# Scores joined over two halves of the key positions, a rewritten routing and placement, and all gathers of the combine issued first

## What is computed

```python
# MLA, per head: 128 "nope" features and 64 "rope" features, causal softmax over 1024 keys
s = (einsum('bqhd,bkhd->bhqk', qn, k_nope) + einsum('bqhr,bkr->bhqk', qp, k_pe)) * scale
p = softmax(where(mask, s, -inf));  out = einsum('bhqk,bkhe->bqhe', p, v)
# experts: top group of 4, top 2 experts of its 4; 2048 assignments in all
g_sel = argmax(g_logits);  e_top, e_idx = top_k(e_logits[g_sel], 2)
gate = softmax(g_logits)[g_sel] * softmax(e_top)
expert_id = g_sel * 4 + e_idx
counts = bincount(expert_id);  pad_start = cumsum(pad(counts)) - pad(counts)
dest = pad_start[e] + rank of the assignment within its expert
ys = (silu(xs @ w_gate[e]) * (xs @ w_up[e])) @ w_down[e]    # xs gathered by block
out[tok] = gate0 * ys[dest0] + gate1 * ys[dest1];  result = rms_norm(h + out)
```

## Time and profile before

| | us |
|---|---|
| median of 3 runs | 3902.52 (3900.98 to 3903.48) |
| the profiled execution, own time | 3896.27 |
| its span, first to last instruction | 3895.0 |
| PE busy | 3660.8 (94%) |
| DVE busy | 1771.2 (45%) |
| ACT busy | 1017.9 (26%) |
| POOL busy | 693.2 (18%) |
| mean granted TensorE clock | 0.973 |

### The profile page before, as it was taken

One profiled execution on the slowest core, in us unless ns is written; L12 is line 12 of the kernel. 1 busy time (PEld: TensorE's weight loads), 2 busy tenths in 40 slices (PEclk: granted clock), 3 DMA queues, 4 the chain that ended last, 5 costly groups with the idle time before them and its releaser, 6 DMA issues. The chain is left out here.

```text
span 3895.0 us, 42152 instructions
## 1 busy us (share of the span) xinstructions
PE 3660.8 (94%) x16927; PEld 2372.2 (61%) x16927; DVE 1771.2 (45%) x3356; ACT 1017.9 (26%) x1857; POOL 693.2 (18%) x688
## 2 busy tenths in 40 slices
PE   5999999999999989998999999999898896999994
PEld 4666554777777766665547888888663553333331
DVE  5666754455555536666333334444326633000003
ACT  2444223322222214443223222222120411111111
POOL 1122000110000002211001111000010002555554
PEclk9999899999999999999999999999999997999997
DMA  6010550222222140002411111111400204887524
GB/s 213 29 33 21 190 172 27 68 76 81 80 88 90 51 159 25 25 24 85 151 33 44 44 44 54 44 44 43 132 3 0 94 28 158 311 292 254 204 82 146
DMA packets 226147, 364.55 MB, mean 94 GB/s; under 512 B 54584, under 2 KB 156690, under 8 KB 213664
## 3 DMA queue, kind: packets, MB, share of 16 engines
q1 hardware_dynamic: 175440, 239.22, 18.3%
q0 software_dynamic: 47232, 121.75, 8.8%
q10 hardware_dynamic: 3280, 0.89, 0.1%
HBM read 519.00 MB, written 44.04 MB: 145 GB/s over the span
## 5 line engine op out<-in xcount | busy, mean ns | idle before, releaser
L225 PE MATMUL psum<-arena_r,arena_r 128*128 128x512 f32 x4096 | 1302.5, 397 | 15.7 <-DVE weight_ring_r L1775 14.7
L225 PEld LDWEIGHTS psum<-arena_r,arena_r 128*128 128x128 f32 x4096 | 770.5, 188 | 204.5 <-issue 17.4
L225 PE MATMUL psum<-arena 64*128 64x128 f32 (+9 forms) x4048 | 859.4, 382 | 33.4 <-DVE arena L3074 14.9
L225 PEld LDWEIGHTS psum<-arena 128*128 128x128 f32 (+1 forms) x4048 | 521.7, 194 | 335.8 <-issue 220.6
L1801 DVE TENSOR_TENSOR arena<-arena,psum 128x512 f32<-128x512 f32 x512 | 336.7, 684 | 189.4 <-PE psum L225 189.4
L225 PE MATMUL psum<-weight_ring_r,arena_r 128*128 128x512 f32 x1024 | 410.5, 401 | 0.0
L225 PE MATMUL psum<-arena_r,weight_ring_r 128*128 128x512 f32 x1024 | 398.5, 389 | 0.0
L225 PE MATMUL psum<-arena,weight_ring 128*128 128x512 f32 x768 | 341.1, 604 | 19.7 <-DVE arena L2266 12.6
L1758 POOL TENSOR_TENSOR weight_ring_r<-weight_ring,arena_r 128x1024 fp32r<-128x1024 f32 x64 | 154.7, 2419 | 1129.3 <-ACT arena_r L1708 1129.3
L3186 PE MATMUL psum<-arena 128*64 128x512 f32 x1536 | 341.7, 598 | 3.9 <-DMA arena<-in_expert_w_gate,be_i 2.5
L1792 DVE TENSOR_TENSOR arena_r<-arena,arena_r 128x512 fp32r<-128x512 f32 x128 | 88.5, 691 | 462.8 <-ACT arena_r L1746 462.8
(11 more groups left out here) (378 smaller groups left out, 3343.7 us busy)
## 6 DMA issues: line engine op xcount, KB each, us to landing
weight_ring<-in_w_mlp_up SPq DMA_DIRECT2D x32, 1024.0 KB, 6.3
weight_ring<-in_w_mlp_down SPq DMA_DIRECT2D x32, 1024.0 KB, 4.9
arena<-in_w_ada SPq DMA_DIRECT2D x24, 1024.0 KB, 6.0
arena<-in_w_ada SPq DMA_DIRECT2D x40, 512.0 KB
arena<-in_w_in SPq DMA_DIRECT2D x6, 2048.0 KB, 18.5
tmp_ys<-arena SPq DMA_DIRECT2D x24, 512.0 KB
arena<-in_w_out SPq DMA_DIRECT2D x4, 2048.0 KB, 9.2
arena<-tmp_mixed SPq DMA_DIRECT2D x16, 512.0 KB, 3.3
```

What stands on the lines that cost most here:

```text
L225: i = self.nc.tensor.matmul(out, lhs, rhs, start=start and n == 0, stop=stop and n == len(pairs) - 1)
```

## The change

- In attention the key features `kpeT` of tiles 4 to 7 stand on partitions 64 to 127, and the query features `qpeT` on both halves. `pe_scores` first does the 128-row products of both 512-column parts, then the two 64-row products, one on each half of the rows. `sp_queries` and `sp_first_queries` issue one more transfer per head. In the last tile of a mixer VectorE makes a doubled copy (`first_q`) before TensorE turns it.
- The route drops an operation from each `dve_first_max`, builds `hot` by products of one-hots, sums with one scan over tiles (`upto`), and takes the counts and the places from separate products. The gate weights (`dve_route_gates`) come after the placement. Four tables are made in the route's loop (`dve_route_tables`).
- The placement computes `dest` first and the experts of the blocks after it; `row_hot` is made in two halves; the 16 products are 32 columns wide and write four partial sums on four groups of partitions, which a copy and a product with `fold` add up.
- `pool_experts` gathers the rows of step 0 before the gate weights of step 0.
- The combine issues all 16 gathers first; VectorE takes six tiles before it scales the first.

```diff
     V.rt = A.take(2, MH + 1, HALF_ROPE)
+    V.first_q = V.rt.rearrange("p a h f -> p (a h f)")[:, 0:P]
     A = Area(k.arena, 0)
...
         E.wait_ge(read.at("rot", l, t), made.at("ga", l, t + 1) if more else made.at("q_up", l, t, 1))
-        k.turn([(ps[0][0:ROPE, at(h)], V.pe_rot[:, h, :]) for h in range(MH)]).then_inc(*out.up("turn_qpe", l, t))
+        turned = [(ps[0][0:ROPE, at(h)], V.pe_rot[:, h, :]) for h in range(MH)]
+        if not more:
+            E.wait_ge(read.at("first_q", l))
+            turned[0] = (ps[0][:, at(0)], V.first_q)
+        k.turn(turned).then_inc(*out.up("turn_qpe", l, t))
         E.wait_ge(made.at("qk", l, t + 1) if more else made.at("kv", l, t, 0))
-        k.turn([(ps[1][0:ROPE, 0:P], V.pe_rot[:, MH, :])]).then_inc(*out.up("turn_kpe", l, t))
+        if t < NT // 2:
+            k.turn([(ps[1][0:ROPE, 0:P], V.pe_rot[:, MH, :])]).then_inc(*out.up("turn_kpe", l, t))
+        else:
+            k.turn([(ps[1][:, 0:P], flat(V.pe_rot[:, MH - 1:MH + 1, :]))]).then_inc(*out.up("turn_kpe", l, t))
         if more:
...
         if not more:
-            s.activation(k.att.qpeT[0][0:ROPE, at(t)], k.ps[0][0:ROPE, 0:P], ACT.Copy)
+            s.activation(k.att.qpeT[0][:, at(t)], k.ps[0][:, 0:P], ACT.Copy)
         s.activation(V.qpe_out[0:ROPE].rearrange("p h n -> p (h n)"), k.ps[0][0:ROPE], ACT.Copy).then_inc(*out.up("qpe", l, t))
         E.wait_ge(pe.at("turn_kpe", l, t))
         if more:
             E.wait_ge(pe.at("turn_kd", l, t))
-        s.activation(V.kpeT[0:ROPE, at(t)], k.ps[1][0:ROPE, 0:P], ACT.Copy).then_inc(*out.up("kpe", l, t))
+        r = side(t // (NT // 2))
+        s.activation(V.kpeT[r, at(t)], k.ps[1][r, 0:P], ACT.Copy).then_inc(*out.up("kpe", l, t))
         if more:
             s.activation(V.kdn.rearrange("p g n -> p (g n)"), k.ps[1][:, 256:512], ACT.Copy).then_inc(*out.up("kd", l, t))
...
         v.tensor_tensor(V.pe_rot[:, :, hi], V.pe_rot[:, :, hi], V.rt[:, 1], ALU.add).then_inc(*out.up("rot", l, t))
+        if t == NT - 1:
+            E.wait_ge(out.at("rot", l, t))
+            v.tensor_copy(V.first_q.rearrange("p (a r) -> p a r", a=2), spread(V.pe_rot[:, 0:1, :], P, 2, ROPE)).then_inc(*out.up("first_q", l))
...
     nc.sync.dma_start(V.qT[0][:, 0:n], d["q_all"][0][:, 0:n]).then_inc(*queries_arrived(k, 0).dma())
-    nc.sync.dma_start(V.qpeT[0][0:ROPE, 0:n], d["qpe_all"][0][:, 0:n]).then_inc(*queries_arrived(k, 0).dma(l, 0))
+    nc.sync.dma_start(V.qpeT[0][side(1), 512:n], d["qpe_all"][0][:, 512:n]).then_inc(*queries_arrived(k, 0).dma())
+    nc.sync.dma_start(V.qpeT[0][side(0), 0:n], d["qpe_all"][0][:, 0:n]).then_inc(*queries_arrived(k, 0).dma(l, 0))
 
 
 def sp_queries(k, l, h):
     nc, V, d = k.nc, k.att, k.d
     nc.sync.dma_start(V.qT[h % 2], d["q_all"][h]).then_inc(*queries_arrived(k, h).dma())
-    nc.sync.dma_start(V.qpeT[h % 2][0:ROPE], d["qpe_all"][h]).then_inc(*queries_arrived(k, h).dma(l, h))
+    nc.sync.dma_start(V.qpeT[h % 2][side(1), 512:], d["qpe_all"][h][:, 512:]).then_inc(*queries_arrived(k, h).dma())
+    nc.sync.dma_start(V.qpeT[h % 2][side(0)], d["qpe_all"][h]).then_inc(*queries_arrived(k, h).dma(l, h))
 
 
...
-        hi = min(lo + 512, w)
-        k.mm(sc[:, lo:hi], [(V.qT[h % 2][:, at(qt)], k.kT[:, h, lo:hi])], stop=False)
-        i = k.mm(sc[:, lo:hi], [(V.qpeT[h % 2][0:ROPE, at(qt)], k.kpeT[0:ROPE, lo:hi])], start=False)
+    parts = [slice(lo, min(lo + 512, w)) for lo in range(0, w, 512)]
+    for cols in parts:
+        k.mm(sc[:, cols], [(V.qT[h % 2][:, at(qt)], k.kT[:, h, cols])], stop=False)
+    for a, cols in enumerate(parts):
+        i = k.mm(sc[:, cols], [(V.qpeT[h % 2][side(a), at(qt)], k.kpeT[side(a), cols])], start=False)
     i.then_inc(*S_.att_pe.up("scores", l, n))
...
-    E.wait_ge(S_.rt_dve.at("multi"), S_.rt_dve.at("means", NT - 1))
-    multi = V.multi.rearrange("p t e -> p (t e)")
-    k.mm(k.ps[6][:, 0:NT * NE], [(k.c(K_BEFORE), multi)])
-    k.mm(k.ps[6][:, NT * NE:2 * NT * NE], [(k.c(K_ONE), multi)]).then_inc(*S_.rt_pe.up("before"))
+    E.wait_ge(S_.rt_dve.at("upto"), S_.rt_dve.at("means", NT - 1))
+    k.mm(k.ps[4][:, 0:NE], [(k.c(K_ONE), V.upto[:, :, NT - 1])]).then_inc(*S_.rt_pe.up("counts"))
+    k.mm(k.ps[6][:, 0:P], [(V.less, flat(V.multi)), (k.c(K_ONE), flat(V.upto))]).then_inc(*S_.rt_pe.up("before"))
...
-    s.activation(V.t4, V.t4, ACT.Exp).then_inc(*S_.rt_act.up("g_exp"))
+    s.activation(V.g_exp, V.g_exp, ACT.Exp).then_inc(*E.up())
...
+def dve_first_max(k, val, out_max, out_hot):
+
+    E, v, V = k.dve, k.nc.vector, k.rt
+    iota4 = spread(V.iota4.unsqueeze(1), P, NT, 4)
...
     E.wait_ge(E.last)
-    v.tensor_tensor(tmp, val, wide(out_max, 4), ALU.is_equal).then_inc(*E.up())
-    E.wait_ge(E.last)
-    v.scalar_tensor_tensor(tmp, tmp, -64.0, iota4, ALU.mult, ALU.add).then_inc(*E.up())
-    E.wait_ge(E.last)
-    v.tensor_reduce(out_idx, tmp, AX.X, ALU.min).then_inc(*E.up())
-    E.wait_ge(E.last)
-    v.tensor_scalar_add(out_idx, out_idx, 64.0).then_inc(*E.up())
-    E.wait_ge(E.last)
-    v.tensor_tensor(out_hot, iota4, wide(out_idx, 4), ALU.is_equal).then_inc(*E.up())
+    v.tensor_tensor(V.t4, val, wide(out_max, 4), ALU.is_equal).then_inc(*E.up())
+    E.wait_ge(E.last)
+    v.scalar_tensor_tensor(V.t4, V.t4, -64.0, iota4, ALU.mult, ALU.add).then_inc(*E.up())
+    E.wait_ge(E.last)
+    v.tensor_reduce(V.idx, V.t4, AX.X, ALU.min).then_inc(*E.up())
+    E.wait_ge(E.last)
+    v.scalar_tensor_tensor(out_hot, iota4, -64.0, wide(V.idx, 4), ALU.add, ALU.is_equal).then_inc(*E.up())
+
+
+def dve_route_tables(k):
+
+    E, v, V = k.dve, k.nc.vector, k.rt
+    v.tensor_copy(V.iota4, k.c(K_IOTA, 4))
+    v.tensor_scalar_add(V.less, k.c(K_BEFORE), -1.0)
+    v.tensor_scalar(V.again, spread(k.c(K_IOTA, NT).unsqueeze(1), P, NE, NT), 0.5, None, ALU.is_gt)
+    v.tensor_reduce(V.fold, k.ident().rearrange("p (g b) -> p b g", g=4), AX.X, ALU.add).then_inc(*E.up())
...
+        if t == 2:
+            dve_route_tables(k)
...
+    v.tensor_reduce(V.el, V.ge.rearrange("p t g e -> p t e g"), AX.X, ALU.add).then_inc(*E.up())
+    dve_first_max(k, V.el, V.m1, V.e_hot1)
+    E.wait_ge(E.last)
+    v.scalar_tensor_tensor(V.el, V.e_hot1, -3.0e38, V.el, ALU.mult, ALU.add).then_inc(*E.up())
+    dve_first_max(k, V.el, V.m2, V.e_hot2)
+    E.wait_ge(E.last)
+    for n, e_hot in enumerate((V.e_hot1, V.e_hot2)):
+        v.tensor_tensor(V.hot[:, :, n, :].rearrange("p t (g e) -> p t g e", g=NG), spread(V.g_hot.unsqueeze(3), P, NT, NG, EPG),
+                        spread(e_hot.unsqueeze(2), P, NT, NG, EPG), ALU.mult).then_inc(*E.up())
+    E.wait_ge(E.last)
+    v.tensor_tensor(V.multi.rearrange("p e t -> p t e"), V.hot[:, :, 0, :], V.hot[:, :, 1, :], ALU.add).then_inc(*E.up())
+    E.wait_ge(E.last)
+    v.tensor_tensor_scan(flat(V.upto), flat(V.again), flat(V.multi), 0.0, ALU.mult, ALU.add).then_inc(*S_.rt_dve.up("upto"))
+    v.tensor_tensor(V.g_exp, gl, wide(V.g_max, 4), ALU.subtract).then_inc(*S_.rt_dve.up("g_diff"))
     v.tensor_tensor(V.ex, V.m2, V.m1, ALU.subtract).then_inc(*S_.rt_dve.up("e_diff"))
+
...
-    for n, ids in enumerate((V.id1, V.id2)):
-        v.scalar_tensor_tensor(ids, V.g_idx, float(EPG), ids, ALU.mult, ALU.add).then_inc(*E.up())
-        E.wait_ge(E.last)
-        v.tensor_tensor(V.hot[:, :, n, :], iota16, wide(ids, NE), ALU.is_equal).then_inc(*E.up())
-    E.wait_ge(E.last)
-    v.tensor_tensor(V.multi, V.hot[:, :, 0, :], V.hot[:, :, 1, :], ALU.add).then_inc(*S_.rt_dve.up("multi"))
-    E.wait_ge(S_.rt_pe.at("before"))
-    v.tensor_copy(V.after.rearrange("p a t e -> p (a t e)"), k.ps[6][:, 0:2 * NT * NE]).then_inc(*E.up())
-    for t in range(NT):
-        E.wait_ge(E.last)
-        v.tensor_tensor(V.before[:, t, :], V.after[:, 0, t, :], V.cnt, ALU.add).then_inc(*E.up())
-        v.tensor_tensor(V.cnt, V.cnt, V.after[:, 1, t, :], ALU.add).then_inc(*E.up())
-    for n in range(2):
-        E.wait_ge(E.last)
-        v.tensor_tensor(V.multi, V.hot[:, :, n, :], V.before, ALU.mult).then_inc(*E.up())
-        E.wait_ge(E.last)
-        v.tensor_reduce(V.rank[:, :, n], V.multi, AX.X, ALU.add).then_inc(*E.up())
...
-    E.wait_ge(E.last, S_.rt_pe.at("before"), S_.rt_act.at("e_exp"))
-    v.tensor_scalar(V.pad, R.cnt, 1.0 / BLOCK, (BLOCK - 1) / BLOCK - 0.5 + 0.5 / BLOCK, ALU.mult, ALU.add).then_inc(*E.up())
+    E.wait_ge(S_.rt_pe.at("counts"))
+    v.tensor_scalar(V.pad, k.ps[4][:, 0:NE], 1.0 / BLOCK, (BLOCK - 1) / BLOCK - 0.5 + 0.5 / BLOCK, ALU.mult, ALU.add).then_inc(*E.up())
...
-    v.tensor_scalar_add(V.pad, V.pad, -MAGIC).then_inc(*E.up())
-    E.wait_ge(E.last)
-    v.tensor_scalar_mul(V.pad, V.pad, float(BLOCK)).then_inc(*E.up())
-    E.wait_ge(E.last)
-    v.tensor_tensor_scan(V.end, k.c(K_ONE, NE), V.pad, 0.0, ALU.mult, ALU.add)
+    v.tensor_scalar(V.pad, V.pad, -MAGIC, float(BLOCK), ALU.add, ALU.mult).then_inc(*E.up())
+    E.wait_ge(E.last)
+    v.tensor_tensor_scan(V.end, k.c(K_ONE, NE), V.pad, 0.0, ALU.mult, ALU.add).then_inc(*E.up())
+    E.wait_ge(E.last)
```

(55 more changed lines are left out.)

80 lines of the change are left out of this document (34 added, 46 removed).

## The result

The changed kernel takes 3873.6 us (median of 5, 3869.7 to 3881.2) against 3902.5 before; the ratio is 0.9931, 95% interval [0.9917, 0.9946], so 21 to 32 us less: 28.9 by the medians, 27 by the ratio. The forecast was 34 us less, 3868. The profiled execution took 3872.39 us with a span of 3871.1: 23.9 us less than the profiled one of before. Their busy times come first (page, part 1); TensorE loses 25.6 us of work.

A forecast was written before the change was run, and what follows sets the result against it. TensorE, busy 94% of the span, was taken as the bound, except from last logits to first expert products and in the combine; 23.3 + 5.1 + 6.0 = 34.4 us off 3896.3 gives 3861.9, median 3868, range 3857 to 3884.

The forecast's parts named there:

- VectorE taking over: Rival, attention: VectorE's waits keep TensorE's shorter heads from their full gain; total gain 28 us, 3874; chance 12%.
- GpSimd held in every gather: Rival, combine: each gather waits for VectorE, end as now or 1 us sooner; total gain 29 us, 3873; chance 12%.
- Attention: 23.3 forecast: Part 1: fewer row switches and overlapping 64-row products, less what does not pay, net 23.3 us; bounds 9 and 29.
- The wide step: Attention: two switches fewer save 0.40 us, plus full overlap of the second part; 3.73 us per head.
- The smaller gain beside L416: Attention, tile 7 of four heads whose step before runs L416: 0.65 of 1.25 us taken, 4 x 0.6 lost.
- The extra transfer per head: Attention: queued on SyncE a head ahead of its use; if late, costs at most its landing.
- the fifth: Rival: a transfer or the first tiles give the gain back; under 8 us in all, 3898; chance 3%.
- The second step of layer 1: Attention: L416 waits 3.97 us for its weights and holds the mask, so 1.0 us does not pay.
- Route and experts: 5.1 forecast: Part 2, route and placement: weights no longer wait for tokens, half of up(0) at low clock; 5.1 us, bounds 2 and 6.6.
- Combine: 6.0 forecast: Part 3: gathers first, last output starts 6.6 us sooner, stores give back 0.6; gain 6.0 us, bounds 2 and 8.
- Halves that do not overlap: Rival, attention: row halves do not overlap, attention gives 9 us; total gain 20 us, 3882; chance 12%.
- A clock fall in attention: Rival, attention: half of some 270 us of products at low clock after pauses, 4000 us; chance 2%.

The follow-up runs named there:

- a_onehalf: Changed kernel with both 64-row products of a wide step on the lower half of the array, one after the other: 3874.1 us, ratio 0.9936.
- b_x23: Changed kernel with the two 2 MB loads of x at steps 23 and 26 in layer 0, instead of 16 and 19: 3868.9 us, ratio 0.9914.
- b_fill: Changed kernel with 7 unread 128-column products on constants in TensorE's pause ahead of tile 7's exponential, in each layer: 3875.0 us, ratio 0.9932.
- a_gate1: Changed kernel with the issues for gate(1) ahead of those for down(0): 3872.2 us, ratio 0.9912.
- b_best: Changed kernel with x loads at steps 23 and 26 in layer 0, gate(1) ahead of down(0), first five rsqrts in one pair of operations: 3865.7 us, ratio 0.9907.
- a_rsqrt: Changed kernel with the combine's rsqrts of the first five tiles as one pair of operations on 5 columns: 3874.0 us, ratio 0.9920.

## Why the prediction was right, and where its sizes were off

**The direction and the mechanisms held.** Each part gained, the halves overlap, the route is 15.2 us shorter up to the tokens, all gathers stand in a row. Of the 34.4 us 23.9 came in the profiled execution, and 28.9 between the medians. The time alone would not tell the forecast from its rivals: 3873.6 is what I had written down for VectorE taking over (3874) and for GpSimd held in every gather (3873). That neither happened in that form is shown by the rows.

**Attention: 23.3 forecast, 14.4 found** (5.26 and 9.66, less the 0.50 ahead; 5.2 of the missing 9 are one stop, 3.5 the first heads). The wide step was priced right: 3.76 us in the second head of layer 1 (32.66 to 28.90) for my 3.73, of which 1.56 come with the regrouping and 2.20 with the overlap. (The third head gained 3.31 here and 3.71 in the other executions with these products.) That the 1.56 are the cost of switching between 128 and 64 rows is my reading; a_onehalf shows only that regrouping brings them. The smaller gain beside L416 was right too: 3.10 us in the second head of layer 0 for 3.13. Two terms were wrong.
- *"The extra transfer per head is queued on SyncE a head ahead of its use; were it late it would cost at most its landing."* I looked at the one transfer that the diff adds and not at those already in the queue. TensorE's shorter steps brought the stores' due times forward against 4 MB of x and 1 MB pieces of weights; two buffers could not cover it. The stop and the low clock behind it are 5.2 us, which b_x23 gives back. None of my rivals had it: the fifth named a transfer, but in a size that took nearly all.
- *"The second step of layer 1, where L416 waits 3.97 us for its weights and holds the mask" (1.0).* The wait is in both layers (3.90 us in layer 0 before, 4.04 after), and it fixes a point in time. I had read the earlier trace rows, a stretch of the second and third heads, as attention as a whole: in the first heads TensorE already waited 3.0 and 5.4 us for the exponential before. The first heads gained 1.6 us for 3.1 in layer 0 and 0.1 for 2.1 in layer 1. In layer 0 the waits grew from 3.0 to 6.8 us, so what TensorE won became idle time; this is past the 1 us per head that I had named as a sign of being wrong, in this one head. In layer 1 the waits stayed (5.4 and 5.6 us), and the granted clock fell to 0.62 behind the first of them, where the lowest window of this head before was 0.79. That the transfer and not the clock holds the second step is shown by b_fill; that the low clock took the gain of layer 1 is argued from the windows, not shown. (With the code of before this head took 36.4, 36.5 and 38.4 us, so its gain is itself uncertain by 2 us.)

**Route and experts: 5.1 forecast, 4.3 found.** The walk was right nearly to the step: from the last logits to the end of the tokens' copy it took 16.6 us, forecast 16.3, and 1.69 more to the block experts, forecast 1.5; these came 0.08 us sooner than before and not 0.6. TensorE ended up(0) at 54.1 us behind the last logits, forecast 54.7, but this is two errors that cancel: up(0) started behind the rows of step 1, 2 us later than I had them (44.4 us and not 42.4), and took 7.7 us at a granted clock of 0.91 and not the 9.8 of half low. What was mis-sized is the rest of the transfers: I had them land 53.1 us behind the last logits and they were reported at 55.5. So they and not the clock set gate(1), by 1.4 us. a_gate1 and b_best, in which it is gone, show that this wait is one of queue order.

**Combine: 6.0 forecast, 3.7 found.** The pace of gathers held by VectorE was taken as 1.32 us and was 1.44, 1.8 us over fifteen; the rsqrts as 2.0 and were 2.1, 1.1 us in all. The 0.6 that I let the stores give back was not lost (3.96 us from the last output to the end, 3.97 before). The bounds, 2 and 8, held this execution; over all executions the gain lies between 1.3 and 5.7.

**The rivals.** Halves that do not overlap: refuted by the 1.13 us row. VectorE taking over: partly. Layer 0's quiet heads are 1.55 us longer than layer 1's, but 0.89 of that was there before, and the 0.6 on top was in my sum. GpSimd held in every gather: no, in nine of the sixteen, by up to 0.9 us. A clock fall in attention: it came after pauses, in two or three short stretches per layer, not in half of the stage, and the first head of layer 0 had one before the change too (0.50 from 418 to 426 us).

**Two rules.** The Trainium skill, page "TensorEngine Tiling (Array Packing)", section "PSUM Bottleneck", warned that emptying PSUM may cap a gain on TensorE. The trace agrees in part: the one that stopped TensorE for 2.27 us was ScalarE reading PSUM at L1383, but what held ScalarE was the store of its output buffer in the transfer queue, and not its own work. The Trainium skill's page "SBUF — State Buffer", section "Summary: rules for kernel authors", has the later of GpSimd and a VectorE operation with two SBUF inputs blocked until the first is done. Here an issue of 0.94 us takes up to 1.90 beside VectorE, and in the changed kernel 7 of 16 take 0.95 or less all the same, so the trace agrees in part.

## What to carry to other kernels

Before pricing a faster engine, list what it is handed by due time (loads, and above all stores that free a double buffer) and ask which of these comes first against full transfer engines; a gain ahead of a fixed landing turned in good part into idle time here (1.8 us were left of the 5.3 that the two first heads were to win). An overlap can be right to 3% per head and be worth a fifth in the run, so price a stage by its quiet steps and its fixed points apart. When single repairs are below what runs can tell, stage lengths inside the profile can tell them, if other executions show how much a stage varies by itself: 28.90 us in nearly every quiet head of layer 1, but 47 to 51 in the combine.

## What was not expected of the hardware

- Two 64-row fp32 products of 512 columns on different row halves take 1.13 us, one alone 1.12: full overlap. On one half the pair takes 1.98.
- The granted clock fell (to 0.62 to 0.86 over windows of 6 to 8 us) behind pauses of 2.3 to 3.4 us in a stage in which TensorE is otherwise busy throughout; the stop with a pause of 2.27 us cost 5.2 us in all.
- GpSimd's gather issues vary from 0.93 to 1.90 us with VectorE's sums beside them, and the sum over 16 by 3 us from one execution to the next; with VectorE idle, in one execution, they took 0.93 to 0.95.
- A power (L270) of five columns on GpSimd took 2.04 us in a_rsqrt and 1.20 in b_best; one of one column took 0.55 to 0.57 in some cases and 1.47 to 1.62 in others.
